# Chunks 2 and 3 of a linear-attention output: one trip through scratch memory for both, or one for each

## The reference, cut to what matters

```
o, s_new = hgrn2_chunked(qb, log_f, k_in, ib, s0)
yb = rms_norm(o, o_norm_g) * silu(zb)
g_a, g_b = split(sigmoid(h @ w_merge + b_merge), 2)
y = g_a * (ya @ w_proj_a) + g_b * (yb @ w_proj_b)
out = x + gate * (y @ w_out)
```

## Time and profile before

| | us |
|---|---|
| median of 3 executions | 1565.01 (1562.74 to 1568.99) |
| profiled execution, its own time | 1566.84 |
| its span | 1564.7 |
| PE busy | 1521.3 |
| DVE busy | 813.1 |
| ACT busy | 535.5 |
| POOL busy | 829.1 |

### The profile page before, as it was taken

One profiled execution on the slowest core, in us unless ns is written; L12 is line 12 of the kernel. 1 busy time (PEld: TensorE's weight loads), 2 busy tenths in 40 slices (PEclk: granted clock), 3 DMA queues, 4 the chain that ended last, 5 costly groups with the idle time before them and its releaser, 6 DMA issues.

```text
span 1564.7 us, 31594 instructions
## 1 busy us (share of the span) xinstructions
PE 1521.3 (97%) x12952; PEld 1236.9 (79%) x12952; DVE 813.1 (52%) x1972; ACT 535.5 (34%) x1111; POOL 829.1 (53%) x1074
## 2 busy tenths in 40 slices
PE   5999999899999999999999999999999999999998
PEld 2777788777888777878879878887888977887887
DVE  5766465234558865531444774642353775742122
ACT  4334323434322532334331452233432352243330
POOL 1525433656863643465774482446786363437671
PEclk9999999999999999999999999999999999999999
DMA  9612213534553321453343231353544231243341
GB/s 347 231 55 83 83 56 95 162 110 161 175 195 104 111 71 57 122 148 108 136 162 136 92 119 43 96 121 123 207 155 148 75 109 56 83 122 111 105 166 59
DMA packets 119048, 191.52 MB, mean 122 GB/s; under 512 B 57199, under 2 KB 74952, under 8 KB 118121
## 3 DMA queue, kind: packets, MB, share of 16 engines
q1 hardware_dynamic: 118904, 189.52, 36.8%
HBM read 169.13 MB, written 18.25 MB: 120 GB/s over the span
## 4 chain that ended last, share of the span: by engine, by line
PE 91%; DVE 4%; SPq 1%; POOL 1%; ACT 1%; issue 1%; DMA 1%; DVEq 0%
PE ps_D L799 54%; PE ps_D L796 25%; PE ps_XCD L861 1%; SPq L522 1%; PE ps_XB L937 1%; PE ps_XA L962 1%; PE ps_XA L973 1%; PE ps_XA L999 1%; PE ps_XB L990 1%; PE ps_XB L989 1%; PE ps_XA L937 1%; POOL w_lo_t L1753 1%; DMA th_t<-in_w_ada 1%; PE ps_XB L973 0%; PE ps_XCD L962 0%
## 5 line engine op out<-in xcount | busy, mean ns | idle before, releaser
L1753 POOL TENSOR_TENSOR w_lo_t<-w_raw,w_hi_t 128x256 fp32r<-128x256 f32 x920 | 684.3, 778 | 593.1 <-ACT w_hi_t L1021 592.6
L799 PE MATMUL ps_D<-h_hi_t,w_hi_t 128*128 128x512 f32 x1024 | 409.1, 400 | 0.0
L799 PE MATMUL ps_D<-h_lo_t,w_hi_t 128*128 128x512 f32 x1024 | 399.4, 390 | 0.0
L799 PE MATMUL ps_D<-h_hi_t,w_lo_t 128*128 128x512 f32 x1024 | 399.3, 390 | 0.0
L1021 ACT ACTIVATE w_hi_t<-w_raw 128x1024 fp32r<-128x1024 f32 x232 | 240.3, 1051 | 123.5 <-PE ps_D L796 61.0
L799 PEld LDWEIGHTS ps_D<-h_hi_t,w_hi_t 128*128 128x128 f32 x1024 | 192.2, 188 | 47.7 <-issue 9.8
L799 PEld LDWEIGHTS ps_D<-h_hi_t,w_lo_t 128*128 128x128 f32 x1024 | 192.2, 188 | 41.4
L799 PEld LDWEIGHTS ps_D<-h_lo_t,w_hi_t 128*128 128x128 f32 x1024 | 192.5, 188 | 37.2
L796 PE MATMUL ps_D<-w_hi_t,h_hi_t 128*128 128x384 f32 (+1 forms) x384 | 141.5, 369 | 1.0 <-DVE yf_t L1387 1.0
L796 PE MATMUL ps_D<-w_lo_t,h_hi_t 128*128 128x384 f32 (+1 forms) x384 | 136.5, 356 | 0.0
L796 PE MATMUL ps_D<-w_hi_t,h_lo_t 128*128 128x384 f32 (+1 forms) x384 | 136.2, 355 | 0.0
(11 more groups left out here) (386 smaller groups left out, 2330.4 us busy)
## 6 DMA issues: line engine op xcount, KB each, us to landing
w_raw<-in_w_blocks SPq DMA_DIRECT2D x232, 512.0 KB, 3.4
xr<-in_x_prompt SPq DMA_DIRECT2D x16, 512.0 KB, 5.4
x_or_AT<-in_x_prompt SPq DMA_DIRECT2D x14, 512.0 KB, 5.2
out_dram<-xr SPq DMA_DIRECT2D x12, 512.0 KB, 2.9
z_o<-kk SPq DMA_DIRECT2D x8, 512.0 KB, 3.1
x_or_AT<-in_x_turned SPq DMA_DIRECT2D x3, 1024.0 KB, 5.4
p_or_hf<-in_x_turned SPq DMA_DIRECT2D x3, 1024.0 KB, 5.4
z_k<-kk SPq DMA_DIRECT2D x4, 512.0 KB, 4.6
```

Of the source, the lines that this page charges most:

```text
L799: ins = mm(bank[:, :], w[:, s0, k0 + k, :], a[:, k, :], start=go, stop=end)
L1753: ins = g_.tensor_tensor(w_lo[:, c, k:k + 2], w_raw[:, n % NRAW, k:k + 2], f32(w_hi[:, c, k:k + 2]), ALU.subtract)
```

## The change

The second pair of chunks is taken apart. There are three `onorm` parts instead of two: chunks 0 and 1 (half 60, as before), chunk 2 alone (half 62), chunk 3 alone (half 64). Each has a scratch tensor of its own, a store (`os`), four reads (`ol`) and semaphores of its own. In SP's list the second part's store and reads have the numbers 31.5 and 31.6, the third part's 32 and 32. The halves of `yD` and `yT` stay.

```diff
-O_AT, ON_AT, YD_AT, YT_AT = (57, 59, 61, 63), (60, 64), (65, 66, 69, 70), (66, 67, 70, 71)
-KS_AT, KL_AT, OS_AT, OL_AT = (28, 28), (28, 28), (30, 32), (31, 32)
+O_AT, ON_AT, YD_AT, YT_AT = (57, 59, 61, 63), (60, 62, 64), (65, 66, 69, 70), (66, 67, 70, 71)
+KS_AT, KL_AT, OS_AT, OL_AT = (28, 28), (28, 28), (30, 31.5, 32), (31, 31.6, 32)
+O_PART = (slice(0, 256), slice(256, 384), slice(384, 512))
...
-        o_turned = [t.rearrange("p (h t n) -> p h t n", h=HB, t=2)
-                    for t in (acc_kst[:, :], qq.rearrange("p h n -> p (h n)")[:, 0:1024])]
-        zk, zo = (nc.dram_tensor(f"z_{n}", [2, 4, 32, 2 * HB, 4, 32], F32).ap() for n in "ko")
+        qq_flat = qq.rearrange("p h n -> p (h n)")
+        o_turned = [t.rearrange("p (h t n) -> p h t n", h=HB, n=P)
+                    for t in (acc_kst[:, :], qq_flat[:, 0:512], qq_flat[:, 512:1024])]
+        zk = nc.dram_tensor("z_k", [2, 4, 32, 2 * HB, 4, 32], F32).ap()
+        zo = [nc.dram_tensor(f"z_o{r}", [4, 32, n * HB, 4, 32], F32).ap() for r, n in ((0, 2), (1, 1), (2, 1))]
...
                 elif what == "os":
-                    s.wait_ge("oD", 2 * it + a + 1)
+                    s.wait_ge("oD", 3 * it + a + 1)
                     s.wait_ge(f"ot_in{a}", 64 * it)
-                    load(zo[a].rearrange("i q (h t) j p -> (i q) h (t j p)", t=2), kk[:, :, half], f"oz{a}")
+                    load(zo[a].rearrange("i q (h t) j p -> (i q) h (t j p)", h=HB), kk[:, :, O_PART[a]], f"oz{a}")
...
                 elif task == "onorm":
-                    s.freed(it, "o", 2 * a + 1)
-                    c, half = slice(8 * a, 8 * a + 8), kk[:, :, 256 * a:256 * a + 256]
+                    chunks = ((0, 1), (2,), (3,))[a]
+                    s.freed(it, "o", chunks[-1])
+                    c, part_ = slice(HB * chunks[0], HB * chunks[-1] + HB), kk[:, :, O_PART[a]]
                     do(ts(oss[:, c], oss[:, c], 1.0 / P, EPS, ALU.mult, ALU.add))
                     rsqrt(orst[:, c], oss[:, c], ow1[:, c], ow2[:, c])
-                    for t in (2 * a, 2 * a + 1):
+                    for t in chunks:
                         o = kk[:, :, P * t:P * t + P]
                         s.done(tt(o, o, orst[:, HB * t:HB * t + HB].unsqueeze(2).broadcast_to([P, HB, P]), ALU.mult))
                     s.settle()
-                    do(v.transpose(half, half), "oD")
+                    do(v.transpose(part_, part_), "oD")
                 elif task == "yD":
-                    s.wait_ge(f"ot_in{a // 2}", 64 * (it + 1))
-                    do(stt(yf_slot(16 * it + 4 + a), o_turned[a // 2][:, :, a % 2], og_half[:, 0:1],
+                    r, t = ((0, 0), (0, 1), (1, 0), (2, 0))[a]
+                    s.wait_ge(f"ot_in{r}", 64 * (it + 1))
+                    do(stt(yf_slot(16 * it + 4 + a), o_turned[r][:, :, t], og_half[:, 0:1],
                            szb[:, :, P * a:P * a + P], ALU.mult, ALU.mult), "yt")
```

More of the change, by code:

```diff
@@ L206 @@
         at_half(it, 56, "kD", _r)
-    for _r in range(2):
+    for _r in range(3):
         at_half(it, ON_AT[_r], "onorm", _r)
@@ L267 @@
         + [f"w_in{n}" for n in range(NRAW)] + ["w_hi", "w_lo", "burst", "th_full", "kk", "sq", "ssq", "qa", "k_sc",
-           "lvl", "dgp", "at0", "smax", "p_exp", "p_norm", "kst", "kD", "kz0", "kz1", "kt_in0", "kt_in1", "oD", "oz0", "oz1", "ot_in0", "ot_in1", "yt", "yf", "yh", "yl", "y7f", "y7h", "y7l", "x_in0", "x_in1", "xst", "rstd",
+           "lvl", "dgp", "at0", "smax", "p_exp", "p_norm", "kst", "kD", "kz0", "kz1", "kt_in0", "kt_in1", "oD", "oz0", "oz1", "oz2", "ot_in0", "ot_in1", "ot_in2", "yt", "yf", "yh", "yl", "y7f", "y7h", "y7l", "x_in0", "x_in1", "xst", "rstd",
            "xn", "xm", "xh0", "xh1", "h_hi", "h_lo", "grow", "s_rows", "s_th", "s_sq8", "s_sc", "s_exp", "s_p", "ckv", "s_oT",
@@ L566, in _ @@
                         later.setdefault(b0 + KL_AT[r], []).append(("kl", it, r))
+                for r in range(3):
                     later.setdefault(b0 + OS_AT[r], []).append(("os", it, r))
@@ L603, in event @@
                         load(o_turned[a][32 * j:32 * j + 32].rearrange("p h t (i c) -> p (h t) i c", c=32),
-                             zo[a, :, :, :, j].rearrange("i q n p -> q n i p"), f"ot_in{a}")
+                             zo[a][:, :, :, j].rearrange("i q n p -> q n i p"), f"ot_in{a}")
                 elif what == "xst":
```

## The result

The changed kernel takes 1569.26 us (median of 20 executions, 1566.64 to 1573.94); the kernel before, on the same chips, 1565.13 (20 executions, 1560.11 to 1568.99). The ratio is 1.0027, with an interval of 1.0019 to 1.0036: 0.3% slower, 4.1 us, inside the 0.5% that was called no change and inside the range, but clear of noise. I had put 0.6 us on it. The profiled execution took 1568.33 us (span 1566.2).

A forecast was written before the change was run, and what follows sets the result against it. PE was taken to bound the kernel, busy 1521.3 of 1564.7 us. Terms: 0 for the wait at pb0, 0 for DVE, 0.4 + 0.2 = 0.6 us for SP, so 1565.0 becomes 1565.6 us; range 1561.5 to 1571.5.

The forecast's parts named there:

- the wait at pb0: PE's wait for `yb_lo`, 11.6 us in all: set by ACT's and POOL's split of pa2, not chunk 3's data; gain 0.
- DVE's added work: 15 more small instructions on DVE per iteration, 3.5 us in iteration 1, hidden in DVE's idle time; cost 0.
- The forecast of no visible change: Whole kernel: the split works as meant but is not seen, 1565.6 us against 1565.0; chance 0.86.
- SP's cost: One store and four reads more per iteration on SP delay block loads: 0.4 us in iteration 0, 0.2 in iteration 3.
- the upper bound for that iteration: Iteration 0, SP: stores at 4.84 and read sets at 3.76 us, twice, 17.2 us, make pa1's load 5.6 us late.
- its own signs: Right: four PE waits on `yb_lo`, 11 to 13 us; wrong: under 4 us, or new ACT waits before pa2 over a microsecond.
- the second rival: SP's second round trip delays the load of pa2 (pa1 in iteration 0), up to 11.3 us slower, 1576.3; chance 0.07.
- DVE's in iteration 0: Chunk 2's part on DVE takes about 4.3 us from 275.5, state update 1.25 us late, chunk 3 regains it; cost 0.
- The stores' landing: On SP, each halved store was taken to need 3.1 us to land, as the full store did in iteration 1.
- Chunk 3's transpose: On DVE, half of the joint transpose taken as proportional, 1.25 / 2 = 0.62 us; worth nothing on the path.
- The step from the wait to the time: Late loads at PE priced one for one in kernel time once slack is gone; removing pb0's wait would give 1553.4 us.

The follow-up runs named there:

- it123_only: The kernel before with chunks 2 and 3 taken apart in iterations 1 to 3 only, iteration 0 as before: 1564.55 us, ratio 0.9998.
- late_joint: The kernel before with one number changed, chunk 3's high and low part (yT) at half 70 instead of 71: 1548.12 us, ratio 0.9882.
- it0_only: The kernel before with chunks 2 and 3 taken apart in iteration 0 only, iterations 1 to 3 as before: 1570.25 us, ratio 1.0024.
- late_split: The changed kernel with chunk 3's high and low part (yT) at half 70 instead of 71: 1554.22 us, ratio 0.9923 to the kernel before.

## Why the prediction was right, and where it was off

- *What the wait at pb0 hangs on.* Right, and shown: with chunk 3 one half earlier in ACT's and POOL's order it falls from 11.6 to 0.6 us, and with the chunks apart in three iterations but the order kept (it123_only) it stays at 11.6.
- *DVE's added work is hidden in iterations 1 to 3.* Right (it123_only, 0.9998).
- *The time.* The forecast of no visible change came true, in part by luck. SP's cost was put at 0.6 us and came out near 4; it stayed under the 7.8 us because the slow place is in one iteration of four, and the upper bound for that iteration (5.6 us) had been worked out from SP's transfers alone, not from DVE. By its own signs the forecast is not clean: PE's wait for `yb_lo` is 15.5 us and not 11 to 13, and ACT's wait for a block grew from 1.12 to 5.30 us with pb0's wait, the sign of the second rival, at pa1 instead of pa2. The other signs came: four waits, 64 instructions more, two sets of reads, and in iterations 1 and 3 DVE's wait for scratch memory ahead of chunk 2 is gone; it now waits there for a free `yf` slot, 4.07 us, ended by POOL.
- *The rival of SP's second round trip* was named with its place, pa1's load in iteration 0, and this is what happened, at +3.9 us. I had 0.4 us for it. The term that was mis-sized is DVE's in iteration 0: "small instructions at 0.2 us, as no other stall shows there". Chunk 2's part took from 275.28 to 282.66, 7.4 us instead of 4.3, chunk 3's from 283.85 to 290.30, 6.4 instead of 4.3. So store 3 went at 290.33 and not at 285.7, 4.6 us late; quicker landings gave 1 us back, and pa1's load went at 296.66, 3.6 us behind the forecast. "No other stall shows there" was no evidence: in the kernel before, no small instruction of DVE stood beside those blocks of POOL. I had the sign of it in my own rows, where one such instruction takes 0.65 us, and left it unexplained.
- *The stores' landing*: 3.1 us assumed, 2.5 to 2.7 in iteration 0 (near the 2.6 us of the lower bound), 4.2 and 2.5 in iteration 1, where the sum of the two, 6.7, is near my 6.2. In iteration 3 I had 4.84 twice; it was 4.2 and 3.1. So pa2 there was issued 12.7 us after SP was free (1406.98 to 1419.71), and I had 15.3 (1403.9 to 1419.2).
- *Chunk 3's transpose*: 0.71 us for 0.62, proportion does not quite hold.
- *The step from the wait to the time.* The wait grew by 3.9 us, and the median by 4.1. The forecast priced a wait one for one. That fits between these two kernels, which both have four such waits. It does not fit where waits go altogether: late_joint has 11.0 us of wait less and is 17.8 us faster. The last section shows time lost behind some waits, which the forecast had not counted.

## What to carry to other kernels

A wait is named after what came last, not after what is slow: ask which instructions stand ahead of the awaited one on its own engine before making its data earlier, and try the order first, since it costs one number. When a chain is cut in two so that a part can start sooner, look at what the queue that issues it has next: here a weight load stood behind two round trips. Work that is moved on DVE is to be priced beside what POOL does at that moment, not from a quiet stretch.

## What the hardware showed that I had not expected

PE's wait at pb0 costs more than its length. After some of these waits PE's clock is at its lower level, 1.2 GHz, for a while. In the kernel before, the granted clock right behind the first wait (3.2 us), and then after it (stretch, length, busy time of PE and PEld with counts, DVE, ACT, POOL, then granted clock):

```profile
308.20:314.20 6.00, 6.00 (x14) 4.80 (x15) 0.32 (x1) 0.00 (x0) 2.61 (x4) 0.50 0.20 79
314.50:317.30 2.80, 2.80 (x14) 2.30 (x13) 1.22 (x3) 1.58 (x2) 1.26 (x2) 1.00 0.00 0
```

14 matmuls in 6.0 us at 0.50, then 14 in 2.8 us at 1.00: about 3 us lost on top of a wait of 3.2. In the changed kernel, behind the longer wait of 7.1 us:

```profile
311.80:314.60 2.80, 2.74 (x7) 2.20 (x8) 0.00 (x0) 0.00 (x0) 2.69 (x4) 0.50 0.44 170
315.00:317.80 2.80, 2.80 (x14) 2.29 (x13) 1.38 (x2) 0.00 (x0) 0.00 (x0) 1.00 0.00 0
```

Here the low level holds for 2.8 us, 7 matmuls, and then the clock is back. So what a wait adds is not in proportion to its length: the shorter wait was followed by the longer low stretch. Over all the traces a wait of the same length, 3.19 us, is followed by no matmul at the low level or by 5 to 12 (a matmul then takes 0.63 us instead of 0.39), and a wait of 2.0 by none or by 6 to 8.

At the full level matmuls start 0.23 us apart, at the low one 0.43. From the start of pb0 to the start of its 21st matmul, against 20 such steps at the full level, the kernel before loses 2.9, 0.1, 1.6 and 1.7 us in its four iterations, 6.3 in all; the changed one 1.4, 1.7, 1.7 and 0.1, 4.9 in all; late_joint 0.2 in all, late_split 2.6.

This accounts for most of what late_joint gained beyond the wait: 11.0 us of wait and 6.1 of clock are 17.1 of the 17.8 us between the medians (18.9 between the spans of the profiled executions). It also accounts for over half of the gap between two numbers above: the wait grew by 3.9 us and the profiled executions' spans by only 1.5, and 1.4 of the missing 2.4 us are the changed kernel's shorter low stretches. Which wait draws a low stretch differs from trace to trace, so a single profile's span is no measure of the change. The medians are better: among the 27 executions of the kernel before that ran beside it0_only, the fastest (1560.17 us) has a mean granted clock of 0.997 and the slowest (1569.77) of 0.989. What decides whether the clock falls behind a wait was not tried.
